# The prologue of a two-block transformer kernel in order of arrival, and the second gate's modulation at the second norm

## The reference

```python
def modulation(cond, w, bias):
    m = jax.nn.silu(cond) @ w + bias
    return jnp.split(m, 3, axis=-1)
...
        sx, scx, gx = (m[:, None, :] for m in modulation(c, ada_w[i], ada_b[i]))
        sc, scc, gc = modulation(c_ctx, ada_w[i], ada_b[i])
        hx = rms_norm(x, norm_g[i]) * (1 + scx) + sx
        hc = rms_norm(ctx, norm_g[i]) * (1 + scc) + sc
...
        x = x + gx * yx
```

## Time and profile before

| | us |
|---|---|
| three runs | 2292.14, 2299.05, 4334.81 |
| median | 2299.05 |
| the profiled execution | 2295.94 |
| its span, first to last instruction | 2294.2 |
| TensorE busy in it (matmuls) | 1988.2 (87%) |
| VectorE busy | 1100.2 (48%) |
| ACT busy | 885.9 (39%) |
| GpSimd busy | 697.5 (30%) |

### The profile page before, as it was taken

One profiled execution on the slowest core, in us unless ns is written; L12 is line 12 of the kernel. 1 busy time (PEld: TensorE's weight loads), 2 busy tenths in 40 slices (PEclk: granted clock), 3 DMA queues, 4 the chain that ended last, 5 costly groups with the idle time before them and its releaser, 6 DMA issues.

```text
span 2294.2 us, 27444 instructions
## 1 busy us (share of the span) xinstructions
PE 1988.2 (87%) x10708; PEld 1599.2 (70%) x10708; DVE 1100.2 (48%) x1621; ACT 885.9 (39%) x1199; POOL 697.5 (30%) x310
## 2 busy tenths in 40 slices
PE   4899999999697887883974799999979989999997
PEld 3787777777576776762763588788758866878875
DVE  3322666663375855857797333223233433421332
ACT  3253656563335344343222344234332323422432
POOL 1121010103113313231253244444424442444442
PEclk9999999999888998886996899999989999999998
DMA  7121212122101011021111232333223231323331
GB/s 274 36 65 44 75 48 92 47 84 74 58 28 46 28 37 47 19 69 60 55 46 37 65 92 92 92 94 99 83 58 108 83 100 55 92 93 100 92 92 46
DMA packets 46256, 166.79 MB, mean 73 GB/s; under 512 B 5392, under 2 KB 5520, under 8 KB 45872
## 3 DMA queue, kind: packets, MB, share of 16 engines
q1 hardware_dynamic: 44208, 158.88, 22.2%
q10 hardware_dynamic: 1920, 6.16, 0.7%
HBM read 162.92 MB, written 2.10 MB: 72 GB/s over the span
## 4 chain that ended last, share of the span: by engine, by line
PE 71%; DVE 20%; ACT 5%; issue 2%; DMA 1%; POOL 0%; ACTq 0%; DVEq 0%
PE ps L447 19%; PE ps L449 19%; PE ps L448 19%; PE ps L552 4%; DVE ex L1183 2%; PE ps L565 2%; PE ps L582 2%; DVE sq L1183 2%; DVE hf L1183 2%; DVE acc L1183 2%; ACT sq L822 1%; DVE Alo L1183 1%; DVE hf L1189 1%; DVE tmp L1183 1%; ACT ex L822 1%
## 5 line engine op out<-in xcount | busy, mean ns | idle before, releaser
L1167 POOL TENSOR_TENSOR wlo<-raw,whi 128x1024 fp32r<-128x1024 f32 x251 | 609.8, 2443 | 1343.2 <-ACT whi L805 1343.2
L805 ACT ACTIVATE whi<-raw 128x1024 fp32r<-128x1024 f32 x251 | 257.6, 1055 | 709.1 <-PE ps L449 687.2
L447 PE MATMUL ps<-Ahi,whi 128*128 128x512 f32 x1200 | 484.3, 404 | 41.8 <-issue 23.8
L449 PE MATMUL ps<-Ahi,wlo 128*128 128x512 f32 x1200 | 474.2, 395 | 0.0
L448 PE MATMUL ps<-Alo,whi 128*128 128x512 f32 x1200 | 472.9, 394 | 0.0
L447 PEld LDWEIGHTS ps<-Ahi,whi 128*128 128x128 f32 x1200 | 232.0, 193 | 111.3 <-issue 38.8
L1189 DVE SCALAR_TENSOR_TENSOR cv<-ps,vec,cv 128x511 f32<-128x511 f32 (+1 forms) x176 | 131.9, 749 | 318.2 <-ACT cv L822 313.6
L449 PEld LDWEIGHTS ps<-Ahi,wlo 128*128 128x128 f32 x1200 | 231.7, 193 | 51.4
L448 PEld LDWEIGHTS ps<-Alo,whi 128*128 128x128 f32 x1200 | 232.4, 194 | 47.4 <-issue 0.2
L447 PE MATMUL ps<-Fhi,whi 128*128 128x512 f32 x416 | 166.7, 401 | 12.5 <-DVE Flo L1183 12.5
L448 PE MATMUL ps<-Flo,whi 128*128 128x512 f32 x416 | 164.5, 396 | 0.0
(11 more groups left out here) (233 smaller groups left out, 3341.2 us busy)
## 6 DMA issues: line engine op xcount, KB each, us to landing
raw<-in_units SPq DMA_DIRECT2D x299, 512.0 KB, 3.7
X<-in_xT ACTq DMA_DIRECT2D x1, 2048.0 KB, 12.8
out_xT<-X SPq DMA_DIRECT2D x8, 256.0 KB, 2.1
CX<-in_ctxT ACTq DMA_DIRECT2D x1, 1024.0 KB, 15.6
masks<-in_masks ACTq DMA_DIRECT2D x1, 512.0 KB, 3.5
acc<-in_rope ACTq DMA_DIRECT2D x1, 384.0 KB, 3.1
gmw<-in_gmw ACTq DMA_DIRECT2D x1, 384.0 KB, 2.9
bs<-in_bs ACTq DMA_DIRECT2D x1, 384.0 KB, 3.8
```

The lines of the kernel that those rows point to most:

```text
L447: nc.tensor.matmul(out, sh, mh, start=first, stop=False)
L449: return nc.tensor.matmul(out, sl, mh, start=False, stop=last)
L805: nc.scalar.activation(whi[:, s % CONV, :], raw[:, c % RAW, :], ACT.Copy).then_inc(sem("whi"), 1)
L1167: nc.gpsimd.tensor_tensor(wlo[:, s % CONV, :], raw[:, plan.unit_at[("split", s)] % RAW, :], whi[:, s % CONV, :].bitcast(fp32), ALU.subtrac ...
```

## The change

It does six things.

1. X and CX are loaded in four pieces each (two row blocks), on SP's queue between the units; ACT waits for each piece, and for `vec` alone before cnd. The table load in front of the first root goes.
2. The order of the modulation tiles is a list, `ADA`: shift and scale of the same rows stand side by side.
3. VectorE's sums and modulated rows stand between the tiles; the sum over partitions is TensorE's behind tile 3 (`SS_AFTER`).
4. `modulated` makes (X × scale) × rstd in one operation, and the shift is added by ACT in its copy to `hi` (`shifted`, two activations) and by VectorE in `low` (two operations).
5. Of the 16 tiles in the attention 12 stay; those at q = 0 of pairs 1, 2, 3 and at q = 4 of pair 7 go.
6. The last four (`ada` 20 to 23, the gate of layer 1) are three in front of the second norm's sum and one behind it, with `arow` in `sq`; their transposes follow, and VectorE adds their bias behind rows 4 to 7.

The core of the diff; left out are the renaming of tiles and the same edits a second time.

```diff
 LOG_EXP = "natural_log_exp_and_others"
+ADA = [(0, 0), (0, 4), (0, 1), (0, 5), (0, 2), (0, 6), (0, 3), (0, 7)]
+ADA += [(0, j) for j in range(8, 12)] + [(1, j) for j in range(12)]
+ADA_BESIDE = {(p, q): i + 8 for i, (p, q) in enumerate([(0, 0), (0, 4), (1, 4), (2, 4), (3, 4), (4, 0), (4, 4), (5, 0),
+                                                        (5, 4), (6, 0), (6, 4), (7, 0)])}
+SS_AFTER = 3
+INPUTS_AT = {2: 0, 4: 1, 5: 2, 6: 3}
 GV_AT, GG_AT = [0, 1, 2], [3, 4]
 BACK = 5
 SX_AT = [[0, 1, 2], [3, 4, 5], [6, 7]]
...
-                ada_t(0, j - 1)
-        ada_t(0, 7)
-        norm("n0")
+        for i in range(8):
+            ada(i)
+            if i:
+                ada_t(i - 1)
+            if i == SS_AFTER:
+                norm("n0")
...
+                    ada_t(ADA_BESIDE[p, q // 4 * 4], slots=[3])
         out(PAIRS - 1, TN - 1)
         for m in range(8):
             tile(("l0", m), [("residc", m + 1)], ktiles("wout0", m))
 
+        for i in range(20, 23):
+            ada(i)
         norm("n1")
+        ada(23)
+        for i in range(20, 24):
+            ada_t(i)
         tile("r", [("gr", 1)], ktiles("gr", 0))
         def decay(h, d):
             tile((("gf", "gb")[d], h), [("g_min", 2 * h + d + 1), ("g_log", 6 * h + 3 * d + 1)])
...
         Q, K = (place(28672 + 3072 * i, n, [2, 2, N]) for i, n in enumerate(["Q", "K"]))
-        Pr, PT, arow = sq, hf, rstd
+        Pr, PT = sq, hf
+        arow0 = place(2560, "arow0", [2, 2 * P])
+        arow1 = sq[:, :, :].rearrange("p a t -> p (a t)")
+
+        def arow(i):
+            return (arow0[:, i % 2, :] if i < 8 else rstd[:, i % 2 * 2 * P:(i % 2 + 1) * 2 * P] if i < 20 else
+                    arow1[:, (i - 20) * 2 * P:(i - 19) * 2 * P])
+
         small = place(34816, "small", [3, 8])
...
+                if c in INPUTS_AT:
+                    two = slice(2 * INPUTS_AT[c], 2 * INPUTS_AT[c] + 2)
+                    sy.dma_start(X[:, two, :], a["xT"][:, two, :]).then_inc(sem(f"in{INPUTS_AT[c]}"), 16)
+                    sy.dma_start(CX[:, two, :], a["ctxT"][:, two, :]).then_inc(sem(f"in{INPUTS_AT[c]}"), 16)
                 if c >= RAW:
...
-                ada(0, j)
-                if j == 0:
-                    pe.wait_ge(sem("consts"), 16 * 4)
+            for i in range(8):
+                ada(i)
+                if i == 0:
+                    pe.wait_ge(sem("consts"), 16 * 3)
+                    pe.wait_ge(sem("ones"), 2)
                 else:
-                    ada_t(0, j - 1)
-            ada_t(0, 7)
-            pe.wait_ge(sem("ones"), 2)
-            norm("n0")
+                    ada_t(i - 1)
+                if i == SS_AFTER:
+                    norm("n0")
+            ada_t(7)
...
+            for i in range(20, 23):
+                ada(i)
             norm("n1")
+            ada(23)
+            for i in range(20, 24):
+                ada_t(i)
             tile("r")
             done(linear("r", Ahi, Alo, 0, SAT["n1"] + 1, BOTH))
             def queries(h):
...
-            for name in ("vec", "ident"):
-                t = {"vec": vec, "ident": ident}[name]
-                ac.dma_start(t[:, :], a[name]).then_inc(sem("consts"), 16)
+            ac.dma_start(vec[:, :], a["vec"]).then_inc(sem("vec"), 16)
+            ac.dma_start(sel[:, :], a["sel"]).then_inc(sem("consts"), 16)
             ac.dma_start(eps1[:, :], a["eps1"]).then_inc(sem("consts"), 16)
-            ac.dma_start(sel[:, :], a["sel"]).then_inc(sem("consts"), 16)
-            ac.dma_start(X[:, :, :], a["xT"]).then_inc(sem("xl"), 16)
-            ac.dma_start(CX[:, :, :], a["ctxT"]).then_inc(sem("cl"), 16)
-            nc.scalar.preload_act_table_set(LOG_EXP)
+            ac.dma_start(ident[:, :], a["ident"]).then_inc(sem("consts"), 16)
             do = Serial(ac, sem, "act")
...
-            ac.wait_ge(sem("consts"), 64)
+            ac.wait_ge(sem("vec"), 16)
             ac.wait_ge(sem("cz"), 1)
...
-            squares("n0", both, lambda k: [])
-            root("n0")
+            def shifted(layer, dst):
+
+                ac.wait_ge(sem("hf"), split[0] + 1)
+                k, b = dst
+                for c, cols in enumerate([slice(0, T), slice(T, N)]):
+                    act(b[:, k, cols], hf[:, split[0] % 2, cols], ACT.Identity, mod[:, layer, 2 * k + c:2 * k + c + 1], 1.0,
+                        "hi" if c else None)
+                split[0] += 1
+
+            squares("n0", both, lambda k: [(f"in{k // 2}", 32)])
+            ac.wait_ge(sem("consts"), 48)
+            root("n0", False)
             for k in range(KD):
-                high(Hhi[:, k, :])
+                shifted(0, (k, Hhi))
...
             for k in range(KD):
-                high(Ahi[:, k, :])
...
-            def sums(name):
+            def sums(name, ks=None):
                 i = NI[name]
                 _, k_, _, n = NORMS[i]
                 per = 2 if name in ("n0", "n1") else 1
                 if i:
 
                     ve.wait_ge(sem("psum"), plan.index[("ss", NORMS[i - 1][0])] + 1)
-                for k in range(1, k_):
+                for k in ks or range(1, k_):
                     ve.wait_ge(sem("n_sq"), nsq[0] + per * (k + 1))
                     g = NK[i] + k
                     first = sq[:, (g - 1) % 3, 0:n] if k == 1 else acc[:, 0:n]
                     tt(acc[:, 0:n], first, sq[:, g % 3, 0:n], ADD, "n_acc")
-                nsq[0] += per * k_
+                if ks is None or k == k_ - 1:
+                    nsq[0] += per * k_
 
             made, waiting = [0], []
...
+                dst, i, shift = waiting.pop(0)
                 hi, lo = dst
                 ve.wait_ge(sem("hi"), i + 1)
-                tt(lo, hf[:, i % 2, 0:lo.shape[-1]], hi.bitcast(fp32), SUB, "lo")
+                if shift is None:
+                    tt(lo, hf[:, i % 2, 0:lo.shape[-1]], hi.bitcast(fp32), SUB, "lo")
+                else:
+                    for c, cols in enumerate([slice(0, T), slice(T, N)]):
+                        stt(lo[:, cols], hf[:, i % 2, cols], shift[:, c:c + 1], hi[:, cols].bitcast(fp32), ADD, SUB,
+                            "lo" if c else None)
 
...
 
-            def modulated(name, layer, hi, lo):
-                i = NI[name]
-                ve.wait_ge(sem("n_rs"), 2 * i + 2)
-                for k in range(KD):
-                    b = to_split(N)
-                    for c, (src, s) in enumerate([(X, slice(0, T)), (CX, slice(T, N))]):
-                        tt(b[:, s], src[:, k, :], rstd[:, s], MUL)
-                        ts(b[:, s], b[:, s], sc1[:, layer, 2 * k + c:2 * k + c + 1], mod[:, layer, 2 * k + c:2 * k + c + 1],
-                           MUL, ADD, s="hf" if c else None)
...
-            def ada_t(layer, j):
-                ps = psum(("adaT", layer, j))
+            def modulated(layer, k, hi, lo):
+                b = to_split(N)
+                for c, (src, cols) in enumerate([(X, slice(0, T)), (CX, slice(T, N))]):
+                    stt(b[:, cols], src[:, k, :], sc1[:, layer, 2 * k + c:2 * k + c + 1], rstd[:, cols], MUL, MUL,
+                        "hf" if c else None)
+                queued(hi[:, k, :], lo[:, k, :], mod[:, layer, 2 * k:2 * k + 2])
+
+            def ada(i):
+                ps = psum(("ada", i))
+                do(nc.vector.tensor_copy(arow(i), ps[:, 0:2 * P]), "arow")
+
+            def ada_t(i):
+                layer, j = ADA[i]
+                ps = psum(("adaT", i))
                 tt(mod[:, layer, 4 * j:4 * j + 4], ps[:, 0:4], v_(f"ada_b{layer}", 4 * j, 4), ADD, "mod")
-
-            def scales(layer):
-                stt(sc1[:, layer, :], mod[:, layer, 16:32], 1.0, v_(f"norm_g{layer}", 0, 16), ADD, MUL)
+                if 4 <= j < 8:
+                    c = slice(4 * j - 16, 4 * j - 12)
+                    stt(sc1[:, layer, c], mod[:, layer, 4 * j:4 * j + 4], 1.0, v_(f"norm_g{layer}", 4 * j - 16, 4), ADD, MUL)
 
             do(nc.vector.memset(cnd[:, :, :], 0.0), "cz")
             do(nc.vector.memset(ones[:, :], 1.0), "ones")
             do(nc.vector.memset(small2[:, :], 0.0), "ones")
-            ve.wait_ge(sem("consts"), 64)
-            sums("n0")
-            for j in range(8):
-                ada(0, j)
-                if j:
-                    ada_t(0, j - 1)
-            ada_t(0, 7)
-            scales(0)
-            modulated("n0", 0, Hhi, Hlo)
+            ve.wait_ge(sem("vec"), 16)
+            ada(0)
+            sums("n0", [1])
+            ada(1)
+            ada_t(0)
+            sums("n0", [2, 3])
+            ada(2)
+            ada_t(1)
+            sums("n0", [4, 5])
+            sums("n0", [6, 7])
+            ada(3)
+            ada_t(2)
+            ada(4)
+            ada_t(3)
+            ve.wait_ge(sem("n_rs"), 2)
+            for i in range(5, 9):
+                modulated(0, i - 5, Hhi, Hlo)
+                if i < 8:
+                    ada(i)
+                ada_t(i - 1)
+            for k in range(4, 8):
```

(67 more changed lines are left out.)

24 lines of the change are left out of this document (9 added, 15 removed).

## The result

| | us |
|---|---|
| before, median of 4 runs beside it | 2297.89 |
| changed kernel, median of 4 runs | 2273.16 |
| ratio, 95% interval | 0.9898 (0.9876 to 0.992) |
| changed kernel again (z0 below), on the chip of z1 to z3 | 2274.78, ratio 0.9901 (0.9886 to 0.9917) |
| its profiled execution, span | 2267.79, 2266.1 |

The median of before takes in one run of 4334.81 us; without it the median is 2296.72, and the ratio leaves it out.

The account below looks back on a forecast made before the run. TensorE was taken to hold 71% of the chain of waits and VectorE 20%. Gains of 16 (prologue), 8 (attention) and 3 (second norm) make 27 off 2295.94: 2269 us, with 8 in 10 for 2258 to 2283.

Parts of the forecast that it names:

- Arrival: Prologue: with inputs in pieces between units, unit 7 lands about 21.9 us and modulated rows start at 29.6, not 53.48.
- Rows: Modulated rows on VectorE: cheaper operations take 2.59 us per k against 3.21.
- The late split: Prologue: c0's weight is converted only behind all eight shifted rows, so c0 starts at 57.0 us, against 60.96.
- The prologue as a whole: From the start to c0's end at 67.1 us: gain 16.0 us, bounds 11 to 20.
- part 4: Second norm: three modulation tiles hidden before its sum, one behind; gq0 starts at 643.5 us; gain 3 us (0 to 5).
- Attention: Four of sixteen modulation tiles leave the attention, where TensorE is the limit: gain 8 us (5 to 9.6).
- 2.7, three times, is 8.1: Attention: each of the three tiles removed at q = 0 costs TensorE 2.7 us, with its transpose.
- a sign of being wrong: Attention: waits for hf in pairs 1 to 3 would show the forecast wrong; no size given.
- fillers as cover: Attention rival: the removed tiles' time becomes waits for VectorE's copies, so nothing is gained; total 2277 us, chance 0.10.
- The fourth tile: Attention, pair 7: the tile costs 1.5 us, but TensorE waits around it already, so removal gains 0.3.
- TensorE at the high level in the prologue: Prologue rival: a tile takes 1.08 us instead of 1.93, 5 us less on the chain; total 2264 us, chance 0.08.
- Pieces that don't overlap: Prologue rival: loads in SP's queue run one behind the other, c0 ends at 118 us; total 2321 us, chance 0.03.

Follow-up runs that it names:

- z0: The changed kernel run again unaltered: median 2274.78 us, ratio 0.9901 to the kernel before.
- z1: Changed kernel with c0's weight unit converted behind the third shifted row, and TensorE starting c0 only after five lo rows: 2267.47 us.
- z3: The program of x2 run again, on the chip of z0: 2265.71 us.
- x3: Changed kernel with X and CX loaded whole on ACT's queue again, not in pieces: 2281.16 us.
- x4: Changed kernel with VectorE's four operations per row block, ACT's single copy and VectorE's single subtraction restored: 2282.96 us.
- x2: Changed kernel with ACT converting c0's weight unit behind the fourth shifted row of the first norm, not behind all eight: 2265.81 us.
- x1: Changed kernel with all sixteen modulation tiles back in the attention and none around the second norm: 2279.87 us.
- z2: x2 with gq0's weight unit also converted in front of the second norm's roots, not behind eight shifted rows: 2266.27 us.

## Why the prediction was right, and where it was off

**Arrival.** Tile 0 ran from 5.7 us and the squares kept up. Tile 3 waited for its first unit until 22.4 and ended at 24.7, 1.8 later than forecast; the tiles behind the sum ran at the high level and gave 1.2 back; an addition and a scale in front of the first row, which the sum had left out, took 0.5: rows from 30.7, not 29.6. That trace was the earliest: in nine others with the sum behind tile 3 and the inputs in pieces the first row starts between 30.9 and 32.3.

The Trainium skill (DMA: Bandwidth & Descriptors, section Bandwidth) says to batch DMAs to 1 MiB or more for 75% of peak, behind a table with one time for each transfer size. Such a loss did not show in this queue: with the inputs in pieces of 256 and 512 KB it moved 388 GB/s, with loads of 2 and 1 MB 413 (x3) and 414 (before), and x3 is slower all the same.

**Rows.** 2.6 us per k, 22.8 for all with their waits (22.6 forecast). x4 confirms the term.

**The late split** was named as next, with its place and sum: c0 at 57.0 forecast, 58.6 measured, 1.3 of that from the rows. x2 shows that it is a cause, worth 6.6 us at c1.

**The prologue as a whole** gained 15.2 by the first tile (12.0 by z0's trace), 16.0 forecast. That the two are so near is in part luck. The prediction took 82.30 for c1's start in the kernel before, but that row is c0's eighth k-step: c1 stood at 84.14, already at the high level, so its own end of c0, 67.1, meant a gain of 17.0. c0 ended 1.9 later than forecast. The same slip is in part 4, where 646.19 is the eighth k-step of r and gq0 stood at 647.72.

**Attention.** The step that was mis-sized is "2.7, three times, is 8.1". Each of pairs 1 to 3 became 2.4 us shorter (from the tile at q = 4 to the next, 37.0 to 37.1, not 39.45), and pair 4, which has its tile at q = 0 again, 0.4 longer: 6.6 by the last transpose at q = 2. What the sum put at nothing is the wait for `hf` of 0.6 us in each of the three pairs, the very thing that the prediction had named as a sign of being wrong. So the rival's mechanism, fillers as cover, is real but small. I had taken the place at q = 0 as free of it because no wait showed there; beside a filler it can't.

The fourth tile, forecast 0.3, gave nothing that can be seen: from the last transpose at q = 2 to the first output tile x1, which has it, needs 16.6 us, and the kernels without it 16.5 to 17.5. Before needs 14.9. Most of the difference is in one group of 24 matmuls, which has waited 1.64 us in both:

```profile
524.85 1.53 PE L565 MATMUL ps<-hf,V 128*64 128x128 f32 x24 [1.64 <-DVE hf L1348]
```

```profile
503.60 2.83 PE L588 MATMUL ps<-hf,V 128*64 128x128 f32 x24 [1.64 <-DVE hf L1395]
```

The granted clock over it is 1.00 before and 0.50, the level of 1.2 GHz, in the changed kernel; why is not shown. The eight output tiles behind gave it back in that trace, at 8.21 us each and not 8.43. In z0 they took 8.43, and pair 4 took 1.3 us more than in the first trace, at a granted clock of 0.84 from 392 to 403: z0 gained 3.4 in this stage, not 6.5.

**Second norm.** Forecast 3, measured 3.5 between sum and gq0, with r behind the addition of row 4 and gq0 behind wlo as said. By the right row of before gq0's start was forecast 4.2 us nearer to the sum and came 3.6 nearer. z2 shows that moving gq0's conversion wins nothing: late it costs 1.0 us of waiting, and early 1.3.

**The rivals.** TensorE at the high level in the prologue came true for three tiles only (28.4 to about 36), and c0's first 4 us were low. Pieces that don't overlap: no.

**The sum.** The terms measured, 25 by the first trace and 19 by z0's, stand around the 24.7 (22.6 for z0) by which the medians fell; 27 was forecast. Of the 4.2 us between 2269 and 2273.16, 2.0 are the base: the forecast is counted from the profiled execution's 2295.94, and before's median beside the changed kernel is 2297.89. The rest is mostly the attention (8, not 6.6 to 6.9) and the prologue (16, not 15.2).

## What to carry to other kernels

When one stage starts sooner, look at what else is issued by the same engine behind its last step, here a weight's conversion behind eight copies; put it where its partner rests. A reordering is judged with that mended: here the same interleaving was worth nothing that could be measured, or 7 us. Before two kernels are ranked by a stage of one trace, compare the granted clock and the spacing of the same matmuls in it. And an operation of VectorE that reads two SBUF operands, set beside GpSimd's subtraction of two, is added to it and not overlapped (2.62 us, not 0.48, beside 2.34).
